# Attention values on two column groups of 64, softmax sums from GpSimd pair sums and ones products, and a reordered beginning

## The reference

```python
def attend(q, keys, vals, scale):
    s = jnp.einsum('bqhgd,bkhd->bhgqk', q, keys) * scale
    p = jax.nn.softmax(s.astype(jnp.float32), axis=-1).astype(vals.dtype)
    return jnp.einsum('bhgqk,bkhe->bqhge', p, vals)
...
y = latent_attention(q, k, v, kc, vc, scale).reshape(z.shape) * jax.nn.silu(z)
```

## Time and profile before

| What | Value |
|---|---|
| median of 3 runs | 1052.6 us (1052.39 to 1053.06) |
| profiled execution | 1052.06 us, span 1050.1 us |
| granted TensorE clock, mean | 0.971 |
| TensorE busy | 963.9 us, 92% |
| VectorE busy | 510.0 us, 49% |
| ScalarE busy | 421.4 us, 40% |
| GpSimd busy | 136.5 us, 13% |
| chain that ended last | TensorE 81%, VectorE 7%, ScalarE 4% |
| its first line | `pv`, line 1692, 10% of the span |

### The profile page before, as it was taken

One profiled execution on the slowest core, in us unless ns is written; L12 is line 12 of the kernel. 1 busy time (PEld: TensorE's weight loads), 2 busy tenths in 40 slices (PEclk: granted clock), 3 DMA queues, 4 the chain that ended last, 5 costly groups with the idle time before them and its releaser, 6 DMA issues.

```text
span 1050.1 us, 12554 instructions
## 1 busy us (share of the span) xinstructions
PE 963.9 (92%) x4563; PEld 668.7 (64%) x4563; DVE 510.0 (49%) x872; ACT 421.4 (40%) x753; POOL 136.5 (13%) x158
## 2 busy tenths in 40 slices
PE   2789999999899999899899889899997999999896
PEld 2468889888465455455478677689774545445475
DVE  2535534532864444556452563543548444555443
ACT  4424433322113554656831432533321244555902
POOL 3000000001250001000640200000013300100720
PEclk9899999999889999999999899899999899999998
DMA  9802220311300232022053211130513000022022
GB/s 331 282 16 65 62 75 6 101 41 47 114 1 1 94 130 97 1 81 81 1 172 73 81 30 51 43 98 1 137 40 126 1 0 1 1 81 80 1 100 81
DMA packets 67867, 74.12 MB, mean 71 GB/s; under 512 B 6148, under 2 KB 47456, under 8 KB 67680
## 3 DMA queue, kind: packets, MB, share of 16 engines
q1 hardware_dynamic: 61392, 60.17, 18.2%
q0 software_dynamic: 4016, 12.77, 3.4%
q10 hardware_dynamic: 2400, 0.38, 0.2%
HBM read 69.11 MB, written 4.19 MB: 70 GB/s over the span
## 4 chain that ended last, share of the span: by engine, by line
PE 81%; DVE 7%; ACT 4%; issue 3%; DMA 2%; POOL 1%; ACTq 1%; DVEq 0%; POOLq 0%
PE pv L1692 10%; PE bank L1483 9%; PE bank L1484 9%; PE bank L1485 8%; PE bank L1743 6%; PE bank L1653 3%; PE bank L1774 3%; PE bank L1776 3%; PE bank L1775 3%; PE bank L1620 2%; PE bank L1600 2%; DMA W<-in_w_in 2%; PE bank L1669 2%; PE bank L1521 2%; PE bank L1523 2%
## 5 line engine op out<-in xcount | busy, mean ns | idle before, releaser
L1483 PE MATMUL bank<-hA_parts,W_parts 128*128 128x512 f32 (+1 forms) x496 | 181.7, 366 | 11.7 <-DVE h_low_parts L1016 9.1
L1484 PE MATMUL bank<-hA_parts,W_parts 128*128 128x512 f32 (+1 forms) x496 | 175.2, 353 | 0.0
L894 ACT ACTIVATE hA<-bank 128x512 f32<-128x512 f32 (+1 forms) x168 | 92.5, 561 | 82.1 <-PE bank L1743 56.1
L1290 DVE TENSOR_REDUCE mxp<-bank 128x1 f32<-128x384 f32 x192 | 96.4, 550 | 47.4 <-PE bank L1653 47.1
L1483 PEld LDWEIGHTS bank<-hA_parts,W_parts 128*128 128x128 f32 x496 | 95.7, 193 | 30.8 <-issue 14.0
L1485 PE MATMUL bank<-h_low_parts,W_parts 128*128 128x512 f32 (+1 forms) x310 | 109.9, 354 | 0.0
L1484 PEld LDWEIGHTS bank<-hA_parts,W_parts 128*128 128x128 f32 x496 | 95.6, 193 | 13.7 <-issue 2.2
L1692 PE MATMUL pv<-hA,vg 128*128 128x512 f32 (+1 forms) x168 | 83.1, 576 | 6.8 <-ACT hA L894 6.4
L1692 PE MATMUL pv<-hA,XA 128*128 128x512 f32 (+1 forms) x168 | 81.0, 563 | 2.4 <-ACT hA L894 2.3
L1023 DVE TENSOR_TENSOR W_parts<-W,W_parts 128x1024 fp32r<-128x1024 f32 x44 | 53.5, 1221 | 32.9 <-ACT W_parts L631 32.8
L1308 DVE SCALAR_TENSOR_TENSOR hA<-pv,hA 64x512 f32<-64x512 f32 (+1 forms) x36 | 21.6, 599 | 90.8 <-ACT hA L837 90.6
(11 more groups left out here) (254 smaller groups left out, 1836.6 us busy)
## 6 DMA issues: line engine op xcount, KB each, us to landing
W<-in_w_in SPq DMA_DIRECT2D x39, 512.0 KB, 4.0
W<-in_w_mod SPq DMA_DIRECT2D x8, 2048.0 KB, 8.0
W<-in_w_out SPq DMA_DIRECT2D x4, 2048.0 KB, 7.8
gqk<-in_w_mod SPq DMA_DIRECT2D x2, 1536.0 KB, 10.5
cqkv<-in_w_mod SPq DMA_DIRECT2D x2, 1536.0 KB, 14.7
XA<-in_x SPq DMA_DIRECT2D x4, 512.0 KB, 7.7
XA<-in_x POOLq DMA_DIRECT2D x4, 512.0 KB, 6.6
x_between_layers<-XA POOLq DMA_DIRECT2D x4, 512.0 KB, 2.9
```

The costliest lines, as they stand in the source:

```text
L894: act.activation(prob[slot % 4][:, 0:nq], ps("sc", l, h, q0, kt)[:, 0:nq], ACT.Exp, scale=MLA_SCALE if h < MLA_H else GQA_SCALE)\
L1290: dve.tensor_reduce(mxp[:, t, half:half + 1], ps("mx", l, h, q0, t, half)[:, 0:384], AX, ALU.max).then_inc(*up("part_max", l, h, q0, t, half))
L1483: pe.matmul(p[:, 0:c[1]], high[:, k, :], h_hi[:, k, toks], start=(k == 0), stop=False)
L1484: pe.matmul(p[:, 0:c[1]], low[:, k, :], h_hi[:, k, toks], start=False, stop=False)
```

## The change

**Values.** `vm` and `vg` lose their ones and hold 64 columns per head. A value product becomes two, each with the same 64 value columns as its stationary operand and half the queries: the first writes partitions 0 to 63, the second 64 to 127 of one bank. A head has one bank, its context queries in columns 256 on, its latent queries in columns 0 to 255. A head waits for `o_scaled` of the head two before.

**Sums.** GpSimd adds the probabilities of two neighbouring key tiles (`add_pair`), four additions per head in layer 0 and three in layer 1. TensorE multiplies ones with the pair sums in the same two column groups (`den`), at unit 2 of the next head; for the last head behind the first four steps of the first output tile. `recip` is one pair of instructions per head, behind unit 3 of the next head, and both `normalise` blocks move into `maxima`, before tile 3 in layer 0 and tile 4 in layer 1. There are six `prob` buffers instead of four, and an exponential waits for the pair sum of the buffer's former content too.

**Around them.** GpSimd's `round_k`, paddings, additions and `w_lo` are put in one order by heads. `w_high` of the first half moves to heads 8 to 10, one piece at a time, that of the second half behind `y_high`. `x_back` is issued by SyncE ahead of the first `w_out` block. The maxima of GQA heads use `q_both` and all 128 rows of `k_twice`.

**Beginning.** The identity is loaded first, the tiles of `x` come before the vector rows, the condition uses exponentials and a logarithm in place of the tanh, and block 3 of `w_mod` and its turn come one step earlier.

```diff
-        vm = XA[:, 0:3456].rearrange("p (t r c) -> p t r c", t=TILES, r=3)
+        vm = XA[:, 0:2304].rearrange("p (t h v) -> p t h v", t=TILES, h=MLA_H)
...
+                def add_pair(h, q0, nq, i, slot):
+
+                    pool.wait_ge(*at("prob", l, slot + 1))
+                    if head_before(l, h, 1):
+                        pool.wait_ge(*at("filled", "den", *head_before(l, h, 1)))
+                    pool.tensor_tensor(pair_sum[q0][i], prob[slot % PROBS][:, 0:nq],
+                                       prob[(slot + 1) % PROBS][:, 0:nq], ALU.add)\
+                        .then_inc(*up("pair_sum", l, h, q0, i))
...
+                slot = 0
+                for h in heads:
+                    if h + 1 < MLA_H:
+                        round_k(l, h + 1)
+                    if h in (MLA_H - 1, MLA_H):
+                        b = h + 1 - MLA_H
+                        pool.wait_ge(*at("filled", "sc", l, MLA_H + b - 2, 256, TILES - 1))
...
+                        pool.memset(q_high[b][64:96, :].bitcast(F32), 0.0).then_inc(*up("q_pad", l, b))
...
+                    for q0, nq, nk in qbs(l):
+                        for i in range(nk // P // 2):
+                            add_pair(h, q0, nq, i, slot)
+                            slot += 2
+                            if q0 and 3 * (h - 9) + i in range(KD):
+                                weights_low(0, (3 * (h - 9) + i,))
+                weights_low(1, range(KD))
...
-                        if slot >= 4:
-                            act.wait_ge(*at(*prob_reader(l, slot - 4)))
+                        if slot >= PROBS:
+                            act.wait_ge(*at(*prob_reader(l, slot - PROBS)))
+                            act.wait_ge(*at("pair_sum", *pair_of(l, slot - PROBS)))
...
-                        if j == 0 and h:
-                            recip(h - 1, *qbs(l)[-1][:2])
+                        if j == 3 and h:
+                            recip(h - 1)
...
                     for q0, nq, nk in qbs(l):
                         for t in range(q0 // P, (q0 + nq) // P):
+                            if t == (3 if l < DEPTH - 1 else 4):
+                                for block in normal:
+                                    normalise(*block)
...
+                    for e in range(2):
+                        half = slice(64 * e, 64 * e + 64)
+                        dve.scalar_tensor_tensor(out=un[r:r + 64, n2 * e:n2 * e + n2], in0=pv_banks[h % 2][half, cols],
+                                                 scalar=0.5, in1=rd[half, cols], op0=ALU.mult, op1=ALU.mult)\
+                            .then_inc(*up("o_scaled", l, h, q0))
...
-                if k in (0, 2):
-                    mod(0, 2 + k // 2)
-                if k in (1, 3):
-                    mod_turn(0, 2 + k // 2)
+                if k == 0:
+                    mod(0, 2)
+                if k == 1:
+                    mod_turn(0, 2)
+                    mod(0, 3)
+                if k == 2:
+                    mod_turn(0, 3)
...
-                    mm = pe.matmul(pv_banks[i % 2][:, 0:nq], v, prob[sl % 4][:, 0:nq], start=(kt == 0),
-                                   stop=(kt == nkt - 1))
+                    o, n2 = pv_banks[h % 2][:, half_cols(q0, nq)], nq // 2
+                    for e in range(2):
+                        mm = pe.matmul(o[64 * e:64 * e + 64], v, prob[sl % PROBS][:, n2 * e:n2 * e + n2],
+                                       start=(kt == 0), stop=(kt == nkt - 1), skip_group_check=True)
...
+                def den(h):
+
+                    p = open_("den", l, h)
+                    for q0, nq, nk in qbs(l):
+                        cols, n2, n = half_cols(q0, nq), nq // 2, nk // P // 2
+                        for i in range(n):
+                            pe.wait_ge(*at("pair_sum", l, h, q0, i))
+                            for e in range(2):
+                                mm = pe.matmul(p[64 * e:64 * e + 64, cols], ones[:, 0:64],
+                                               pair_sum[q0][i][:, n2 * e:n2 * e + n2], start=(i == 0), stop=(i == n - 1),
+                                               skip_group_check=True)
+                    close(mm, "den", l, h)
...
                         flush(2)
+                        if j == 2 and h:
+                            den(h - 1)
```

More of the change, by code:

```diff
@@ L214, in build @@
         qh = [hA[:, 2 * i * T:(2 * i + 1) * T] for i in range(2)]
-        prob = [hA[:, 3072 + 512 * i:3584 + 512 * i] for i in range(4)]
-        rd, un = hA[:, 5120:5632], hA[:, 5632:6144]
+        rd, un = hA[:, 5120:5504], hA[:, 5632:6144]
         Ab = [[hA[:, o + 512 * d:o + 512 * d + 512].rearrange("p (h t) -> p h t", h=4) for d in range(2)]
@@ L349, in turned_bank, with pair_of @@
             return pv_banks[1] if l == 0 else ps("modT", l, b)
+        def pair_of(l, slot):
+            h, u = divmod(slot, sum(nk // P for _, _, nk in qbs(l)))
+            ctx_units = 2 if l < DEPTH - 1 else 0
+            return (l, h, 0, 0) if u < ctx_units else (l, h, 256, (u - ctx_units) // 2)
         def prob_reader(l, slot):
@@ L412, in _ @@
                 for i in range(IN_AFTER[l] + 2, IN_AFTER[l + 1] + 2 if l + 1 < DEPTH else len(W_SEQ)):
+                    if i == W_POS[("out", l, 0)]:
+                        sp.wait_ge(*at("pv_filled", l, MLA_H - 1, 256))
+                        if l:
+                            sp.wait_ge(*at("x_saved", l - 1))
+                        for t in out_tiles(l):
+                            src = x_dram[(t - 2) * P:(t - 1) * P, :] if l else a["ctx"][0, t * P:(t + 1) * P, :] \
+                                if t < 2 else a["x"][0, (t - 2) * P:(t - 1) * P, :]
+                            sp.dma_start(X[:, t, :], src).then_inc(*dma("x_back", l))
                     block_dma(i)
@@ L876, in _ @@
                 slot = 0
-                recips = [] if l == 0 else [(0, heads[-1], 256)]
                 neg_max(0)
@@ L918, in _ @@
                             y_high((0, 1))
-                        c = j - 3 if h == heads[-2] else j + len(todo) - 4 if h == heads[-1] and j else -1
-                        if 0 <= c < KD:
-                            w_high(2 * c // KD, (2 * c % KD, 2 * c % KD + 1))
-                        if j == 3 and len(qbs(l)) == 2:
-                            recip(h, *qbs(l)[0][:2])
+                        u = j - len(todo) + TILES
+                        if h in (8, 9, 10) and (h, u) in W_HIGH_AT:
+                            w_high(0, (W_HIGH_AT.index((h, u)),))
                     if more:
@@ L928, in _ @@
                 y_high((2, 3))
-                recip(heads[-1], *qbs(l)[-1][:2])
+                recip(heads[-1])
                 act.wait_ge(*at("y_attn", l, heads[-2], 256))
@@ L934, in _ @@
                 y_high((6, 7))
+                w_high(1, range(KD))
             x_rstd(DEPTH, list(range(2, TILES)))
@@ L1007, in _ @@
                     turned_copy(t - 1)
+            condition()
             turned_copy(TILES - 1)
@@ L1083, in _ @@
                             src = ps("tok", l, t)[:, 256:384].rearrange("p (g v) -> p g v", g=2)
-                            for half in range(2):
-                                dve.tensor_copy(vg[:, t, :, 128 * half:128 * half + 64], src)\
-                                    .then_inc(*up("vg", l, t, half))
-                            let_go(("tok", l, t), "vg", l, t, 1)
+                            dve.tensor_copy(vg[:, t, :, :], src).then_inc(*up("vg", l, t))
+                            let_go(("tok", l, t), "vg", l, t)
                     elif item == "ga":
@@ L1367, in _ @@
                         low_parts(h + 1)
-                    if len(qbs(l)) == 2:
-                        normalise(h, *qbs(l)[0][:2])
+                    normal = [(h - 1, *b[:2]) for b in qbs(l)] if h else []
                     if h + 1 < len(heads):
-                        maxima(h + 1)
+                        maxima(h + 1, normal)
+                    else:
+                        for block in normal:
+                            normalise(*block)
                 y_low(range(4))
-                normalise(heads[-1], *qbs(l)[-1][:2])
+                for q0, nq, nk in qbs(l):
+                    normalise(heads[-1], q0, nq)
                 y_low(range(4, KD))
@@ L1784, in _ @@
                             out_products(p, t, range(4))
+                            if t == todo[0]:
+                                den(heads[-1])
                         for t, p in ahead:
```

203 lines of the change are left out of this document (92 added, 111 removed).

## The result

The changed kernel takes 1072.64 us (1070.66 to 1072.95, 4 runs), the kernel before 1052.49 in the same comparison (1051.78 to 1053.06): ratio 1.0188, 95% interval 1.017 to 1.0205, slower by 20 us. Its profiled execution took 1072.9 us with a span of 1071.1. The range held the time and the sign was right, but the sum was +11.1 and the time came out at +20, so the table asks where the rest is. It sets the start of the turns of row maxima (`max_rows`, the first record of each head, rounded to 0.1 us) in the two traces against the terms of the forecast.

What follows compares the result with a forecast made beforehand. TensorE was taken to bound the MLA heads, and a chain through VectorE to end each GQA head. Terms +9.8 +3.4 +5.3 -0.5 -3.4 -3 -0.5 gave +11.1 on 1052.06: 1063 us, range 1046 to 1075.

Steps and rivals of the forecast that it cites:

- The visit: Each TensorE entry into and exit from the split array costs 0.35 us; 168 for the value units, 58.5 us.
- The rival of a free visit: Split array gives its factor two, entering and leaving cost nothing: 1019 us, chance 0.10.
- The MLA heads: Five heads of layer 0 at +1.29 us and five of layer 1 at +0.81: +9.8 in both layers.
- all on the path, as TensorE is full: In the MLA heads of both layers, the whole +9.8 us of TensorE work lengthens the kernel.
- The GQA heads of layer 0: Heads 6 to 10, walked along VectorE's chain and TensorE's work: +3.4 us, including GpSimd's slowing of VectorE.
- +0.6 for GpSimd: In the GQA heads of layer 0, GpSimd gets in VectorE's way: 0.6 us, within that stage's +3.4.
- The GQA heads of layer 1: Three plain heads +2.7 us together, two with a `w_mod` block +1.3 each: +5.3.
- Last heads: Last head of each layer up to its output products: -0.5 us in layer 0, -3.4 in layer 1.
- GpSimd no longer runs `w_lo` beside it: In layer 1's last head, the output products' waits for `y_low`, 2.0 us, go.
- The beginning: Start of the kernel, with new load order and `w_mod` block 3 earlier: -3 us, bounds -5.5 and +1.
- the +2 against it: At the beginning, TensorE idles before the block at 32 us, which then runs at half clock: +2 us.
- GpSimd slows VectorE throughout: Rival: GpSimd bounds heads 9 to 11 or slows VectorE; ten heads +0.7 to 1.2 more: 1070 to 1076, chance 0.12.

Runs made afterwards that it cites:

- twos: The changed kernel with value units run two at a time, so split-array entries fall from 168 to 84, every product kept: 1056.01 us.
- whole products: The changed kernel with each value pair replaced by one product of all 128 columns, sums still in the split array: 1078.65 us.
- The filler: The changed kernel with four unneeded TensorE products before the turn of the row maxima in heads 7 to 11 of both layers: 1065.06 us.
- short additions: The changed kernel with GpSimd's pair additions cut to 16 columns from head 1 of each layer on: 1062.32 us.
- short additions and normalise behind: The changed kernel with GpSimd's additions cut to 16 columns from head 1 on and both `normalise` blocks moved behind VectorE's joining: 1052.17 us.
- the beginning alone: The kernel before with only the change's new beginning, nothing else: 1047.71 us, ratio 0.9942 to the kernel before.
- normalise behind the joining: The changed kernel with both `normalise` blocks moved from the middle of VectorE's maxima to behind their joining: 1055.37 us.

## Why the prediction came out as it did

**The visit** (0.35 us, 168 of them): right, from rows of 32 and 64 columns elsewhere in the kernel. It reads 0.34 in the chain of twos, and the whole products give the arithmetic back within 0.15 us in each of heads 1 to 3. The rival of a free visit is excluded: it had whole products at 1115 or more.

**The MLA heads** (+9.8, measured +5.4): right for heads 2 and 4 of layer 0, +1.3 and +1.4 against +1.29, and near it for heads 1 to 4 of layer 1, +0.5 to +0.7 against +0.81. Wrong was "all on the path, as TensorE is full" for head 5: its period didn't grow in layer 0 and fell by 0.6 in layer 1. The rows show the slack, TensorE of the kernel before busy 15.07 of 16.90 us between the turns of heads 5 and 6, and 12.66 of 14.60 in layer 1:

```profile
421.50:438.40 16.90, 15.07 (x48) 7.87 (x48) 9.49 (x18) 10.73 (x19) 0.73 (x1) 1.00 0.00 0
905.20:919.80 14.60, 12.66 (x36) 5.94 (x36) 7.81 (x14) 8.40 (x14) 0.73 (x1) 1.00 0.00 1
```

, from 832 to 905 us, covered heads 0 to 4 of layer 1 and nothing of head 5, nor of layer 0; the forecast took it for all MLA heads. Why head 5 of layer 1 got shorter is open. Heads 1 and 3 of layer 0, which also hold key projections, grew by 0.9 for 1.29, which is left open.

**The GQA heads of layer 0** (+3.4, measured +12.7): the step that failed. The forecast named the right chain (VectorE's tiles 0 to 2, normalise, six reductions) and walked it with two sizes too small. For a blocked head it gives 17.6 against 20.3 measured, for the plain head 9 14.3 against 16.7. Normalise takes 3.5 us from its start at 489.05 to 492.57 and not 2.45; 0.8 of that is GpSimd on one product (1.20 us for 0.42 alone), counted in the forecast as "+0.6 for GpSimd" for all heads together instead of per head. Head 6, which has this and no fall of the clock ahead of it, took 15.3 for 14.3. From the joining to the first scores it takes 2.5 us and not 1.3, as the clock is at half; the forecast had no term for the clock there, though it used one for the beginning. The filler puts the clock at 4.7 us of the 9.3 missed, net of its own cost.

**The GQA heads of layer 1** (+5.3, measured +5.4): right in sum, and that by luck. The blocked heads grew by 1.2 and 1.4 for 1.3 and head 9 by 0.9, as foretold, but head 6 fell by 0.4 and head 10 grew by 2.2. In head 10 the product with `Y` met GpSimd's `w_lo` and took 1.74 us for 0.69; with short additions the head takes 11.7 for 12.8.

```profile
998.79 1.74 DVE L1343 TENSOR_TENSOR YA<-hA,YA 64x512 f32<-64x512 f32 x1
```

**Last heads** (-3.9, measured 0.0; the forecast's own terms for layer 1 add up to -3.1 and not -3.4): layer 0 got its shorter way to the output products, 11.4 us from the turn for 13.6; what came behind took 2.5 us more than before, for a lone `den` of 1.85 and 3.4 us more at half clock. In layer 1 the way was to be 2.7 shorter and took 12.8 for 12.3. Two things ate it: the fall of the clock at 1004 us (11.2 without, in the filler kernel) and GpSimd (10.1 with short additions and normalise behind). The forecast let the waits for `y_low` go since "GpSimd no longer runs `w_lo` beside it". It does: the last pieces of `w_lo` stand between the additions, and `y_low` took 4.65 us for four. With short additions it took 2.50.

**The beginning** (-3): its sign right, its size -5.1 alone. The closed idle stretch is the mechanism that it named; the +2 against it, from half clock ahead of it, was not there in the profile of the beginning alone.

**The rivals.** "GpSimd slows VectorE throughout" (0.12) gave 1070 to 1076, and the time lies there. Its mechanism is a part of what happened: short additions take 10.3 us off, falls of the clock among them, but nothing of the heads once normalise is out of the chain. The clock, the other part, no case had.

## What to carry to other kernels

A split of the array has its price per visit, not per product: count how often other work stands between, and put neighbours together (0.35 us a visit here; twos took 12 us out of layer 0 with normalise behind the joining, and cost 6 in layer 1). Where an engine's chain sets the end of each round, keep all that the round doesn't need behind the link that the others wait for; the place of three lines on VectorE was worth 17 of 20 us. And look at what a new wait of TensorE does to its clock: the wait itself was about 1 us, the half speed behind it as much again, and emptying TensorE of work can bring falls of its own (a head of 14.0 us took 16.5 with 0.86 us less to do).

## What the runs showed of the hardware

- TensorE's clock fell to 1.2 GHz for 3.4 us at head ends where TensorE had been busy 2.17 of 3.80 us, and stayed at 2.4 GHz where filler products of no use made that 3.02 of 4.00. More work gave 4.7 us back in these heads.
- Such falls in the stages outside the heads differ between profiles of kernels that are the same there (first turn at 311.2 to 318.1 us with 17 to 37 us at half clock ahead of it). Within one kernel 1044.35 and 1056.58 us go with granted clocks of 0.973 and 0.959, so they can make up most of its spread.
- The price of the split array is additive and the same for value pairs and ones products: 0.15 us in (0.43 to 0.58, 1.51 to 1.66) and 0.20 out (0.35 to 0.55, 0.86 to 1.05).
- VectorE's products and subtractions with two SBUF inputs that began while a GpSimd addition or subtraction ran ended 0.28 us behind its end for 64x256 (1.19 to 1.38 us for 0.42 alone) and 0.55 for 128x512 (up to 1.78 for 0.68); four of 128x512 took 4.65 us for 2.50. Those with an input in PSUM took not longer at all (421 and 422 ns).
